# Pairing the high and low parts of the hidden state in six of eight gating-input slabs, with VectorE adding the two halves of the sum

## The reference

```python
def hybrid_mixer(h, w_in, ...):
    proj = h @ w_in
    (q, k, v, qi, ki, wi, z, xbc, dt_raw, g_attn, g_ssd) = jnp.split(proj, offsets, axis=-1)
    ...
    a = dsa_attention(q, k, v, qi, ki, wi)
    b = mamba2_branch(z, xbc, dt_raw, conv_w, conv_b, dt_bias, a_log, d_skip, norm_w)
    merged = sigmoid(g_attn) * (a @ w_proj_attn) + sigmoid(g_ssd) * (b @ w_proj_ssd)
    return merged @ w_out

def mamba2_branch(z, xbc, ...):
    ...
    y = ssd_scan(xs * dt[..., None], dt * A, bm, cm) + xs * d_skip[:, None]
    y = y.reshape(bsz, seq, SSD_INNER) * jax.nn.silu(z)
    ...
```

## Time and profile before

| | |
|---|---|
| device time, 3 runs | 1670.34, 1669.66, 1670.3 us (median 1670.3) |
| span of the profiled execution | 1667.3 us |
| granted TensorE clock, mean | 0.998 |
| TensorE (PE) busy | 1651.9 us, 99% of the span |
| VectorE (DVE) busy | 1322.5 us, 79% |
| ScalarE (ACT) busy | 1084.7 us, 65% |
| GpSimd (POOL) busy | 756.9 us, 45% |

### The profile page before, as it was taken

One profiled execution on the slowest core, in us unless ns is written; L12 is line 12 of the kernel. 1 busy time (PEld: TensorE's weight loads), 2 busy tenths in 40 slices (PEclk: granted clock), 3 DMA queues, 4 the chain that ended last, 5 costly groups with the idle time before them and its releaser, 6 DMA issues. The chain is left out here.

```text
span 1667.3 us, 28513 instructions
## 1 busy us (share of the span) xinstructions
PE 1651.9 (99%) x10944; PEld 1490.3 (89%) x10944; DVE 1322.5 (79%) x2204; ACT 1084.7 (65%) x1828; POOL 756.9 (45%) x448
## 2 busy tenths in 40 slices
PE   9999999999999999999999999999999999999997
PEld 8998889998888899998788988899999878898887
DVE  7978887495997877885896699778886689579795
ACT  7676666676765584777653776657577665388572
POOL 8631105872010467864664521057675465351113
PEclk9999999999999999999999999999999999999999
DMA  8545646542555555553445456556455335545552
GB/s 307 163 158 188 220 159 197 190 124 92 187 188 191 193 179 188 163 176 123 135 163 190 152 181 213 166 186 200 151 172 175 127 127 177 177 152 200 192 183 84
DMA packets 81239, 287.10 MB, mean 172 GB/s; under 512 B 9168, under 2 KB 9680, under 8 KB 80976
## 3 DMA queue, kind: packets, MB, share of 16 engines
q1 hardware_dynamic: 79776, 282.10, 51.0%
q10 hardware_dynamic: 1328, 3.18, 0.5%
HBM read 283.90 MB, written 1.05 MB: 171 GB/s over the span
## 5 line engine op out<-in xcount | busy, mean ns | idle before, releaser
L565 POOL TENSOR_TENSOR w_lo<-w_raw,w_hi 128x1024 fp32r<-128x1024 f32 (+2 forms) x239 | 569.3, 2402 | 355.3 <-ACT w_hi L1520 276.0
L1520 ACT ACTIVATE w_hi<-w_raw 128x1024 fp32r<-128x1024 f32 (+1 forms) x544 | 543.0, 1033 | 251.1 <-PE lin L798 159.7
L565 DVE TENSOR_TENSOR w_lo<-w_raw,w_hi 128x1024 fp32r<-128x1024 f32 (+1 forms) x305 | 441.7, 1452 | 37.5 <-ACT w_hi L1520 36.3
L796 PE MATMUL lin<-hid_pair,w_hi 128*128 128x256 f32 x1152 | 330.0, 286 | 0.0
L797 PE MATMUL lin<-hid_pair,w_hi 128*128 128x256 f32 x1152 | 325.9, 283 | 0.0
L798 PE MATMUL lin<-hid_pair,w_lo 128*128 128x256 f32 x1152 | 325.9, 283 | 0.0
L796 PEld LDWEIGHTS lin<-hid_pair,w_hi 128*128 128x128 f32 x1152 | 220.9, 192 | 2.2 <-issue 1.4
L797 PEld LDWEIGHTS lin<-hid_pair,w_hi 128*128 128x128 f32 x1152 | 221.0, 192 | 0.3
L798 PEld LDWEIGHTS lin<-hid_pair,w_lo 128*128 128x128 f32 x1152 | 220.9, 192 | 0.0
L574 POOL TENSOR_TENSOR hid_pair<-arena,hid_pair 128x256 fp32r<-128x256 f32 x64 | 56.6, 889 | 289.1 <-ACT std L1595 171.1
L817 PE MATMUL logit<-h_pair,w_hi 128*128 128x512 f32 x540 | 146.7, 392 | 0.0
(11 more groups left out here) (413 smaller groups left out, 3500.8 us busy)
## 6 DMA issues: line engine op xcount, KB each, us to landing
w_raw<-in_upA SPq DMA_DIRECT2D x112, 512.0 KB, 4.4
w_raw<-in_upB SPq DMA_DIRECT2D x64, 512.0 KB, 4.6
w_raw<-in_xbc SPq DMA_DIRECT2D x48, 512.0 KB, 4.3
w_raw<-in_dnA SPq DMA_DIRECT2D x32, 512.0 KB, 4.6
w_raw<-in_dnB SPq DMA_DIRECT2D x32, 512.0 KB, 3.9
w_raw<-in_z SPq DMA_DIRECT2D x32, 512.0 KB, 4.5
w_raw<-in_gates SPq DMA_DIRECT2D x32, 512.0 KB, 4.4
w_raw<-in_ps SPq DMA_DIRECT2D x32, 512.0 KB, 3.9
```

Of the source, the lines that this page charges most:

```text
L565: eng.tensor_tensor(w_lo[slab.slot][:, half, part], w_raw[slab.slot][:, half, part], w_hi[slab.slot][:, half, part].bitcast(F32), ALU.subt ...
L796: nc.tensor.matmul(out, lhs[0], rhs[0], start=first, stop=False)
L1520: nc.scalar.activation(w_hi[slab.slot][:, half, part], w_raw[slab.slot][:, half, part], ACT.Copy)\
```

## The change

`Z_PAIRED = 6`: slabs z0 to z5 of each layer, 12 in all, go through `paired_halves`. Half 0 of the slab is summed in its own bank and half 1 in the bank two places further in the ring. PE therefore waits, before each z slab, for the release of the slab two before it. The new `z_sum(n)` on VectorE adds the high and low sums of each half with one TENSOR_REDUCE (two inputs per result, 512 elements read, 256 written) into `zs` in SBUF, and releases the bank; ACT then applies silu in place, from SBUF to SBUF. On DVE, `z_sum` stands ahead of `stepped` for the even slabs and for u = 0 and 3, and behind `stepped` for the odd slabs of u = 1 and 2. On ACT, the silu of even slabs moves behind the copy of the value product. z6 and z7 keep the plain products and the silu out of PSUM.

```diff
+        Z_PAIRED = 6
+
+        def z_out(slab, half):
+
+            return lin[slab.bank if half == 0 else (slab.bank + 2) % RING][:, :, :]
+
...
-            def paired_halves(slab, n, pairs, wait_chunk):
-
-                outs, last = [down_out(slab, n, half) for half in range(2)], len(pairs) - 1
+            def paired_halves(slab, n, pairs, wait_chunk, outs=None, between=None):
+
+                outs, last = outs or [down_out(slab, n, half) for half in range(2)], len(pairs) - 1
...
                     both_parts(0, k)
+                if between is not None:
+                    between()
                 slab.wait_hi(pe, 1)
...
+                def z_products(n, between=None):
+
+                    slab = slab_at("z", n, l)
+                    slab.ahead(-2).wait_released(pe)
+                    if n < Z_PAIRED:
+                        paired_halves(slab, n, [pairs_of[1 - RAW[2 + l]][:, :, c, :] for c in range(KC)], None,
+                                      outs=[z_out(slab, half) for half in range(2)], between=between)
+                    else:
+                        slab_products(slab, operand, between=between)
...
-                    slab_products(slab_at("z", 2 * u, l), operand)
+                    z_products(2 * u)
...
                     if u in (1, 2):
-                        slab_products(slab_at("z", 2 * u + 1, l), operand, between=lambda: by_token(2 * u + 1))
+                        z_products(2 * u + 1, lambda: by_token(2 * u + 1))
                     else:
-                        slab_products(slab_at("z", 2 * u + 1, l), operand)
+                        z_products(2 * u + 1)
                         by_token(2 * u + 1)
...
                 def z_silu(slab, n):
-                    nc.scalar.activation(zs[:, 2 * n:2 * n + 2, :], lin[slab.bank][:, :, :], ACT.Silu)\
-                        .then_inc(s.bank_free[slab.bank], 1)
+                    if n < Z_PAIRED:
+                        slab.wait_released(act)
+                        nc.scalar.activation(zs[:, 2 * n:2 * n + 2, :], zs[:, 2 * n:2 * n + 2, :], ACT.Silu)
+                    else:
+                        nc.scalar.activation(zs[:, 2 * n:2 * n + 2, :], lin[slab.bank][:, :, :], ACT.Silu)\
+                            .then_inc(s.bank_free[slab.bank], 1)
...
                     done(slab)
-                    z_silu(slab, 2 * u)
                     act.wait_ge(s.da_pv, 4 * l + u + 1)
...
                     nc.scalar.activation(acc[:, u % 2, :, :], tr[:, :], ACT.Copy).then_inc(s.da_out, 1)
+                    z_silu(slab, 2 * u)
...
+                def z_sum(n):
+
+                    if n >= Z_PAIRED:
+                        return
+                    slab = slab_at("z", n, l)
+                    slab.wait_done(dve)
+                    for half in range(2):
+                        bank = z_out(slab, half)
+                        ins = nc.vector.tensor_reduce(zs[:, 2 * n + half, :], bank.rearrange("p a t -> p t a"), AX_X, ALU.add)
+                    ins.then_inc(s.bank_free[slab.bank], 1)
+
...
                     if u < 3:
                         da_probs(u + 1)
+                    z_sum(2 * u)
                     stepped(2 * u)
...
                     weights(slab_at("z", 2 * u + 1, l))
-                    stepped(2 * u + 1)
+                    if u in (1, 2):
+                        stepped(2 * u + 1)
+                    z_sum(2 * u + 1)
+                    if u not in (1, 2):
+                        stepped(2 * u + 1)
```

## The result

| | before | changed |
|---|---|---|
| median of the runs | 1670.03 us (5 runs) | 1675.62 us (5 runs, 1671.87 to 1675.90) |
| ratio to before | | 1.0033 (95% interval 1.0023 to 1.0044) |
| span of the profiled execution | 1667.3 us | 1673.7 us (its own time 1675.69) |
| granted TensorE clock, mean | 0.998 | 0.996 |
| second set of runs (experiment 9) | 1669.24 us | 1676.35 us, ratio 1.0033 (1.0021 to 1.0045) |

In the second set one run of each kernel fell in a slower state (2311.8 us at a granted clock of 0.65 and 2009.3 us at 0.75) and doesn't count.

A forecast was written before the change was run, and what follows sets the result against it. PE, busy 99% of the span, was taken as the bound. Per layer -1.1 gain, +0.9 wait and +2.2 collision gave +2.0, +3.9 for two layers: 1674.2 us, range 1668.8 to 1679.5.

The forecast's parts named there:

- What bounds: z stage: PE is busy 99% of the span, so PE work removed is time gained and each new PE wait is lost.
- PE's gain: z0 to z5: a paired slab takes 5.65 us instead of 5.84, saving 0.19 a slab, 2.3 us for 12.
- VectorE's price: DVE: 24 added reductions of 0.69 us, about 1.3 a pair, costing time only where PE waits for `stepped`.
- Pass 1: Layer walk to `by_token(3)`: `z_sum(1)` delays silu, exponentials and multiplications, `stepped(2)` ends at 747.6, PE waits 0.9 us.
- The collision: Pass 1: POOL's remainder of z5 starts 0.02 before DVE's fourth multiplication, which lasts 2.2 us longer; PE waits 3.1.
- rival 2: Pass 2, `probs(3)` against z7's remainder: a collision there too, 1.9 us a layer, time 1678.0; chance 0.23.
- The sum: Per layer -1.1 gain, +0.9 wait, +2.2 collision: +2.0; two layers +3.9, span 1671.2, time 1674.2 us.
- No collision: Pass 1: the fourth multiplication starts before POOL; -0.2 us a layer, -0.5 in all, time 1669.8; chance 0.26.
- slow reduction: DVE: 1.0 us a reduction, 1.9 a pair; time 1675.7 without a collision, up to 1684 with both; chance 0.12.
- cheap reduction: DVE: 0.42 us a reduction, 0.8 a pair; nothing left of the 0.9 wait, time 1668.0; chance 0.06.
- Bank releases, silus from SBUF: z slabs: releases two slabs back come in time, and silus from SBUF keep their former 0.60 us.

The follow-up runs named there:

- experiment 9: The changed kernel run again for its spread, against the kernel before: 1676.35 us (1670.27 to 1676.56), ratio 1.0033.
- experiment 2: Changed kernel where, in passes 1 and 2, GpSimd starts the remainder of z5 (z7) only after VectorE's multiplications: 1668.91 us, ratio 0.9997 to the kernel before.
- experiment 6: Changed kernel with plain products in all z slabs, VectorE's reductions and ScalarE's silu from SBUF kept: 1669.16 us, ratio 1.0000 to the kernel before.

## Why the prediction was right, and where it was off

- **What bounds.** Right. With PE busy 99% and no wait in the stage, each new wait of PE showed in the time.
- **PE's gain.** Taken 0.19 a slab, 2.3 us; measured 0.90 a layer, that is 0.15 a slab and 1.8 us. It lies within the bounds of 0.11 to 0.27. A paired slab takes 743.49 - 737.81 = 5.68 from its first product, not 5.65, where z0 took 5.84 before; z5, with `by_token` inside it, takes 1.93 + 3.84 = 5.77 without the transposes where z3 took 2.96 + 2.96 = 5.92. The spacing for isolated products in the Trainium skill, TensorE: Matmul & The Clock Gate, Back-to-back issue gap, by which an estimate of 0.5 us were to be had, is further from 1.8 than the rows' 2.3.
- **VectorE's price.** Right: 0.682 a reduction on average (0.69 taken), 1.28 a pair.
- **Pass 1.** The chain `z_sum(1)`, silu, exponentials, multiplications, `z_sum(2)`, `stepped(2)` went as walked; the silu started at 737.57 (737.85 by the walk), the multiplications at 744.22 (744.5). The wait without the collision, forecast at 0.9, is 747.90 - (745.40 + 1.93) = 0.6 in experiment 2. One step matched by another way: the remainder of z3 was taken to run as before, held by POOL from 733.92 to 736.50; it now starts at 734.59, behind `z_sum(0)` and `stepped(0)`, takes 1.68 and ends at 736.27.
- **The collision.** Right in place and size: 3.32 - 1.14 = 2.2, as taken. The margin, forecast as POOL first by 0.02, was 0.01. That the rows of before, which can't resolve 0.02, gave the right winner was luck, and the prediction said as much. The profiles show no coin, though: POOL came first in all eight layers that have the meeting. Whether single runs such as the one of 1670.27 escaped it is not known. Experiment 2 shows the cost and experiment 6 that TensorE's gain takes part. In one reading the shapes were mixed: the four multiplications of 8.92 are of 128x128, and four such take 0.88 alone (732.24 in the trace of before), not 1.14; the 2.2 is the length of one that is held, and it stands.
- **Pass 2** (rival 2). The tie came up and fell the other way by 0.02. The walk had `w_hi` of z7 wait for the exponentials, done 8.7 behind z3's end, with z4's end seen at 8.4. Measured, they were done at 763.54 - 755.17 = 8.4 (763.45 and the 0.09 of pass 1), and z4's end was seen at 763.57 - 755.17 = 8.4, later by 0.03. POOL, which would have been first by 0.01, came 0.02 behind. The first collision came without the second, so that taking this as the less likely case was right, but not for the reason given.
- **The sum.** The step that was off is the sum itself: -1.1 + 0.9 + 2.2 = +2.0 a layer. Measured is +3.4, of which -0.90 is gain and +2.75 wait (3.1 forecast), so far +1.85. The missing 1.6 (1.4 in layer 1) is the granted clock behind the wait, a term that the prediction didn't have at all. The span was forecast at 1671.2 and measured at 1673.7, 2.5 too low. The time was only 1.4 too low, and the difference is luck: the forecast added 3.0 us around the span (the median of three runs less one profiled span of the kernel before), and the profiled run of the changed kernel had 1675.69 - 1673.7 = 2.0 around it. Most runs of both kernels have 1.8 to 2.1.
- **No collision, slow reduction, cheap reduction** (rivals 1, 3, 4). The first is experiment 2, forecast -0.5 against before and measured -0.2 (1668.91 against 1669.09), with an interval that holds both. The others didn't come: 0.68 a reduction.
- **Bank releases, silus from SBUF.** Rightly at nothing: no PE wait names a bank, and all 24 sums and 12 silus from SBUF cost nothing in experiment 6.

## What to carry to other kernels

A change that makes one engine faster moves its neighbours' starts, and an exclusive resource between two of them (here DVE's multiplications and POOL's remainder) can turn a quarter microsecond of shift (0.34 to 0.09 in experiment 6) into 2.2 us of being held; list who will start beside whom before counting the gain. Keep a wait for another engine's new result out of a queue that feeds the critical one: moving the silu of odd slabs off the way to the exponentials turned a loss of 5.6 us into a gain of 1.8. And price a wait of TensorE with the clock that it may lose: a wait of 2.6 us cost 4.0 and 4.2 in the two layers.

## What the runs showed of the hardware

- **TensorE's clock behind an idle stretch.** It stayed at 1.00 behind waits of 0.4, 1.3 and 1.4 us, and it was 0.58 to 0.63 over the 4.0 or 4.1 us behind waits of 2.6 (four of four in two profiles) and 0.66 over the 5.0 us behind one of two waits of 2.4. A fall cost 1.4 to 1.6 us (5.58 and 5.78 instead of 4.20 from `by_token` to the slab's end). No run has a wait between 1.4 and 2.4 at this place.
- **Starts 0.01 to 0.02 us apart decide who is held at SBUF, and the same way in each profile.** POOL 0.01 ahead: VectorE's multiplication of 0.35 lasts 2.5, in eight profiled layers of eight. VectorE 0.02 ahead: POOL's remainder takes 2.58 or 2.59 instead of 2.39, in six of six. The fourth multiplication's free start is worked out from the spacing of 0.263. The Trainium skill, SBUF — State Buffer, Who interferes with whom, has the rule, first come holds it whole; the traces agree.
- **Reductions out of PSUM are not held by POOL**: 1.29 for a pair at 732.80 in the changed kernel while POOL worked from 732.79 to 735.19, and 1.29 again at 755.37, when POOL was idle. The same section of the Trainium skill states it of a tensor_reduce; no row of before could show it.
